# Two pairs of heads scored inside the value unit of the third attention, and its first two probabilities turned together

## Chip, cores and metric

The kernel runs on one core of a Trainium2 chip. The metric is the device time of one launch in microseconds; lower is better. Engines: PE (TensorE, matrix products), DVE (VectorE), ACT (ScalarE), POOL (GpSimd), and SP, whose queue issues the loads of the weights.

## What is computed

A network of two blocks over 256 latent rows and 256 context rows of width 1024, in float32. The first block has two layers; each layer projects the normalised rows, runs three attentions next to each other and merges them. The third one is what the change touches: 16 query heads of width 64 over 4 key heads, with a window of 128 positions and a learned "sink" term in the softmax. Cut to its core:

```python
sq_l, sk_l, sv_l = swa_heads(sq_l, sk_l, sv_l, rope_hd)      # rotated queries and keys, 16 / 4 heads
sq_c, sk_c, sv_c = swa_heads(sq_c, sk_c, sv_c, None)         # the same of the context, not rotated
# latent queries: all context keys, and latent keys within the window
s_loc = jnp.where(mask, jnp.einsum('bqhgd,bkhd->bhgqk', qg, kb), NEG_INF)
s_ctx = jnp.einsum('bqhgd,bkhd->bhgqk', qg, k_ctx)
p_ctx, p_loc = sink_softmax(sink, (s_ctx, s_loc))
o = einsum('bhgqk,bkhd->bqhgd', p_ctx, v_ctx) + einsum('bhgqk,bkhd->bqhgd', p_loc, vb)
# context queries (layer 0 only): context keys alone
(p,) = sink_softmax(sink, (einsum(qg, k_ctx),));  o = einsum(p, v_ctx)
```

The second block (four mixers with large matrix products) is not touched.

## The kernel before

**Order of the work.** `plan()` (lines 163 to 379) writes one list of steps. Each engine's program walks this list and does its own part of each step, in order; semaphores tie the engines together. Nothing is scheduled at run time: an engine that waits holds up all that stands behind it on its queue. The step `gemm` is a unit of matrix product: weights of 256 rows and up to 512 columns at a time (a chunk) are loaded by SP, split into a high part by ACT (line 1749) and a low part by DVE (line 2380), and used by PE in three products (high by high, low by high, high by low; lines 1211 to 1213, 1248 to 1250).

**Banks.** The product memory has eight banks of 128 x 512 float32. PE takes one with `take(pool, key)` (line 1056), which goes round the pool's banks in turn and waits until the bank's last content has been read. The pools overlap:

```python
POOL = {"wide": (0, 1, 2, 3), "turn": (4, 5), "out": (6, 7), "turn4": (4, 5, 6, 7), "out_turned": (6,), "back": (7,)}
```

**In front of the third attention** (lines 285 to 292): the keys `sk`, the queries `sq` in two units of four blocks (two heads each), and the value unit `sv`. The units of kind "rope" leave their result with heads across the partitions. The second, `sq` with j = 1, holds all four banks of "turn4". Their blocks are then rotated one after the other (step `rotate`): ACT writes the swapped halves into a slot of `stage` (line 1815), DVE makes the cosine product (line 2467) and with it gives the bank back, POOL multiplies by the sines and adds (lines 849, 852), ACT makes the high part (line 1823), POOL the low part (line 858). PE meanwhile works on `sv`: four chunks for four row tiles, in the four banks of "wide", and ACT copies these to `v` at the end (line 1897).

**The third attention** (`attend` with r = 2). An item is one query tile and one head; layer 0 has 4 x 16 (the tiles of the context see 256 keys, those of the latent rows 512), layer 1 has 2 x 16 with 512 keys. Per item: scores on PE, two heads at a time in two halves of the array and in two banks (lines 1476, 1479, 1482); the negated row maximum with mask and sink on DVE, in one instruction (line 2925); the exponential with row sum on ACT (line 2171), which gives the bank back; the turning (transposes) of the probabilities on PE (line 1318) into a bank of "turn"; its copy to `probs_turned` on DVE for even items (line 2942) and on ACT for odd ones (line 2192); and the product with V on PE (line 1529) for two heads together. Turnings run LAG = 3 items behind the scores, products with V PV_LAG = 5 behind.

**The start.** The first `FIRST` = 2 items are ahead of the others. PE issues their scores inside `sv`, before its third chunk (line 1174), into "turn4" banks. DVE and ACT have the step `attend_first` for them, which stands ahead of the step of `sv` on their queues. All later items are in the step `attend` behind `sv`, with scores in "wide" banks. So the order on PE, with S01 for the scores of items 0 and 1 and T0 for the turning of item 0, is: two chunks of `sv`, S01, two chunks of `sv`, S23, T0, S45, T1, T2, S67, the first product with V, T3, and so on.

Of the kernel before, what the change touches and what calls it, by code (L numbers as in the profile page):

```python
# [56 lines left out]
LAG = 3  # L57
PV_LAG = LAG + 2
PT_SLOTS = {0: 3, 1: 3, 2: 4}
NM_RING = 32  # L60
FIRST = 2
B_LAG = 3
EARLY_BY = (16, 17)

# [98 lines left out]
def plan():  # L163

    steps, chunks, to_split = [], [], []
# [37 lines left out]
    for l in (0, 1):  # L203
        qt = ALL_TILES if l == 0 else LAT_TILES
# [70 lines left out]
            gemm("value", ("dv", l, j), ALL_TILES, ("h", l), w_in, D, OFF_DV + 512 * j, 512, j=j,  # L275
                 head=(l, 1, qt) if j else None, pool="wide" if j else "turn4")
        scored = len(qt) * HEADS[1]
        steps.append(("attend", l, 1, qt, FIRST, scored))
        steps.append(("head_squares", l, qt[:-1]))
        steps.append(("attend", l, 1, qt, scored))  # L280
        steps.append(("head_squares", l, qt[-1:]))
# [125 lines left out]
def program(nc, dram, out, known):  # L407
    ctx = ExitStack()
    with ctx:
        S = Signals(nc, ctx, known)  # L410
        steps, chunks, to_split = plan()
# [139 lines left out]
        def probs_at(r, i):  # L551

            return stage(i) if r == 1 else STG[:, 512 * ((i + 4) % 6):512 * ((i + 4) % 6) + 512]
# [176 lines left out]
        def squares(t):  # L730

            return QT[:, :, P * t:P * t + P]

        def items(l, r, qt):
            return [(t, h) for t in qt for h in range(HEADS[r])]

# [311 lines left out]
        def _(pe):  # L1048
# [7 lines left out]
            def take(pool, key):  # L1056

                b = POOL[pool][turns[pool] % len(POOL[pool])]
                turns[pool] += 1
                if uses[b]:  # L1060
                    pe.wait_ge(*S.nth(f"bank{b}_emptied", uses[b]))
                uses[b] += 1
                S.use_bank(key, b, uses[b])
                return b
# [78 lines left out]
            def gemm(u, turned):  # L1143
# [27 lines left out]
                for n, (src, k0, kt, col, width) in enumerate(u.chunks):  # L1171
                    while late and late[0][0] <= n:
                        turn(*late.pop(0)[1])
                    if u.more.get("head") and n == (2 if u.key[0] == "sv" else 1):
                        l, r, qt = u.more["head"]
                        attend(l, r, qt, 0, FIRST)
                    if turned and turns_inside(u) and n == len(u.chunks) - 1:
                        turn_qk(turned)
                    if u.more.get("tail") and n in (1, 2):
                        l, r, qt = u.more["tail"]  # L1180
                        done = len(items(l, r, qt))
                        if n == 1:
                            attend(l, r, qt, done, done + LAG)
                        else:
                            attend(l, r, qt, done + LAG, done + PV_LAG)
                    if u.more.get("tail") and n == 3 and u.more["r"] == 2:
                        turn_inverses(u.more["l"])
                    c = u.at[n]
                    pe.wait_ge(*S.at("w_low", c))
                    slot = part_of[c] % PART_SLOTS  # L1190
                    for t in u.tiles:
                        if n == 0:
                            open_banks[t] = take(u.more.get("pool", "wide"), (u.key, t))
                        b = open_banks[t]
                        for kk in range(kt):
                            k = k0 + kk
                            once(left_ready(u.left, k, t))
                            high, low = left_high_low(u.left, k, t)
                            o = banks[b][:, 0:width]
                            if u.more.get("across"):  # L1200
                                a = u.more.get("first", 0)
                                high, low = (part[:, a:512] for part in left_all(u.left, k))
                                block = slice(P * t, P * t + P)
                                o = banks[b][:, a:512]
                                wh, wl = WH[:, slot, kk, block], WL[:, slot, kk, block]
                                pe.matmul(o, wh, high, start=(k == 0), stop=False)  # L1206
                                pe.matmul(o, wh, low, start=False, stop=False)  # L1207
                                mm = pe.matmul(o, wl, high, start=False, stop=(k == u.kt - 1))  # L1208
                                continue
                            wh, wl = WH[:, slot, kk, 0:width], WL[:, slot, kk, 0:width]  # L1210
                            pe.matmul(o, high, wh, start=(k == 0), stop=False)  # L1211
                            pe.matmul(o, high, wl, start=False, stop=False)  # L1212
                            mm = pe.matmul(o, low, wh, start=False, stop=(k == u.kt - 1))  # L1213
                        if n == len(u.chunks) - 1:
                            mm.then_inc(*fills(b))
                            if t == u.tiles[-1]:
                                S.same("w_used", c, f"bank{b}_filled")
                        elif t == u.tiles[-1]:
                            mm.then_inc(*S.up("w_used", c))
# [222 lines left out]
            def attend_first(l, r, qt):  # L1442
                pass

            def attend(l, r, qt, start=FIRST, stop=None):
                todo = items(l, r, qt)
                width = VALUE[r]
                for i in range(start, stop or len(todo)):
                    if r == 0 and i % 2 == 0 and i < len(todo):
                        for n in (i, i + 1):  # L1450
                            t, h = todo[n]
                            nk = P * len(key_tiles(t))
                            qk_ready(l, r, t, h)
                            b = take("turn4" if i < FIRST else "wide", ("s", l, r, t, h, 0))
                            high, low = (part[:, n % 2, :] for part in q_pair(n))
                            k_high, kl = KH[0:MQ, h, 0:nk], mla_k_low(l, h, slice(0, MQ), nk)
                            pe.matmul(banks[b][:, 0:nk], high, k_high, start=True, stop=False)
                            pe.matmul(banks[b][:, 0:nk], low, k_high, start=False, stop=False)
                            pe.matmul(banks[b][:, 0:nk], high, kl, start=False, stop=True).then_inc(*fills(b))
                    if r and i < len(todo):  # L1460
                        t, h = todo[i]
                        nk = P * len(key_tiles(t))
                        qk_ready(l, r, t, h)
                        if r == 1 or h % 2 == 0:
                            halves = [(h, 0), (h, 1)] if r == 1 else [(h, 0), (h + 1, 0)]
                            two = [take("turn4" if i < FIRST else "wide", ("s", l, r, t, hh, m)) for hh, m in halves]
                            hq, hk = (h, h) if r == 1 else (h // 2, h // 4)
                            q_high = QH[:, hq, P * t:P * t + P]
                            ql = q_low(l, r, hq, 1, t).rearrange("p a c -> p (a c)")
# [10 lines left out]
                            for m, b in enumerate(two):  # L1480
                                a = slice(64 * m, 64 * m + 64)
                                pe.matmul(banks[b][:, 0:nk], q_high[a], kl[m], start=False,  # L1482
                                          stop=True).then_inc(*fills(b))
                    if r == 2 and i % 2 == 0 and PV_LAG < i < len(todo):
                        pair_values(l, todo, i - PV_LAG - 1)
                    if LAG <= i < len(todo) + LAG:
                        t, h = todo[i - LAG]
                        pe.wait_ge(*S.at("probs", (l, r, t, h)))
                        pr = probs_at(r, i - LAG)
                        turn(("pt", l, r, t, h), [(pr[:, P * n:P * n + P], P * n) for n in range(len(key_tiles(t)))])  # L1490
                    if r == 2 and i % 2 == 0 and i >= len(todo):
                        pair_values(l, todo, i - PV_LAG - 1)
                    if r < 2 and i >= PV_LAG:
                        n_item = i - PV_LAG
# [227 lines left out]
        def _(act):  # L1722
# [416 lines left out]
            def attend_first(l, r, qt):  # L2139
                if r < 2:  # L2140
                    load_table(ACT.Exp)
                if r == 1:
                    act.wait_ge(*S.at("rope_parted", (("dk", l, 1), 3)))
                attend(l, r, qt, 0, FIRST)

            def attend(l, r, qt, start=FIRST, stop=None):
                todo = items(l, r, qt)
                ring = 4 if r == 1 else 6
                if r == 2 and start:
# [1 line left out]
                for i in range(start, stop or len(todo) + (LAG if r < 2 else PV_LAG + 1)):  # L2151
                    if i == (len(todo) // 2 if l and r < 2 else len(todo)):
                        prepare(by_key[("z", l, r, 0 if r else 1)].pfirst + PART_SLOTS)
                    if r == 2 and i % 8 == 4 and i > 8:
                        save_out(l, *todo[i - PV_LAG])
                    if r == 2 and LAG <= i < len(todo) + LAG and (i - LAG) % 2:
                        turned(l, r, todo, i - LAG)
                    if i < len(todo):
                        t, h = todo[i]
                        nk = P * len(key_tiles(t))  # L2160
# [196 lines left out]
        def _(dve):  # L2357
# [545 lines left out]
                                    SCALE[3] if which == 0 else 1.0, ALU.mult, ALU.mult).then_inc(*S.empties(key))  # L2903

            def attend_first(l, r, qt):
                attend(l, r, qt, 0, FIRST)

            def attend(l, r, qt, start=FIRST, stop=None):
                todo = items(l, r, qt)
                last_in_group = lambda n: todo[n][1] % GROUP[r] == GROUP[r] - 1  # L2910
                for i in range(start, stop or len(todo) + PV_LAG + (2 if r < 2 else 0)):
# [19 lines left out]
                            mx.then_inc(*S.up("neg_max", key))  # L2931
                    if r == 1 and 1 <= i < len(todo):
                        combine(l, i - 1, *todo[i - 1])
                    if r != 1 and LAG <= i < len(todo) + LAG and (i - LAG) % 2 == 0:
                        n = i - LAG
                        t, h = todo[n]
                        key = ("pt", l, r, t, h)
                        nk = P * len(key_tiles(t))
                        if n >= PT_SLOTS[r]:
                            dve.wait_ge(*S.at("pt_used", (l, r, n - PT_SLOTS[r])))  # L2940
                        dve.wait_ge(*S.filled(key))
                        v.tensor_copy(turned_at(r, n)[:, 0:nk], ps(key)[:, 0:nk]).then_inc(*S.empties(key))
# [323 lines left out]
```

## Time and profile before

| | us |
|---|---|
| median of 3 runs (2323.86 to 2324.48) | 2324.48 |
| the profiled execution | 2324.32 |
| its span, first to last instruction | 2322.5 |
| PE busy | 2303.3 |
| DVE busy | 1435.2 |
| ACT busy | 1256.7 |
| POOL busy | 321.0 |

The span is shorter than the execution's time by what lies before the first and behind the last instruction. Busy times overlap, since the engines work side by side. Matmuls are pipelined: one starts before the end of the one before it, so the distance between starts is what one costs, not its duration.

### The profile page before, as it was taken

The page shows a single profiled execution, that of the slowest core. Times are in us where ns is not written, and L with a number is a line of the kernel's source. Part 1 is how long each engine was busy: PE and PEld are TensorE (multiplying, and loading weights), DVE is VectorE, ACT ScalarE, POOL GpSimd, SP SyncE. Part 2 cuts the span into 40 slices and gives each one's busy share as a digit, 9 for nine tenths or more (in the row PEclk, how much of TensorE's full clock was granted, in tenths as well). Part 3 has the DMA queues.
Part 4 walks back from the last instruction along what each step waited for, and adds up shares of the span by engine and source line. Part 5 has one row for each costly group of instructions (what it writes and reads, how often), then busy time and mean ns, then how long its engine had stood idle before and what let it go on. Part 6 is the DMA issues. An engine that isn't in the chain of part 4 may idle for free.

```text
span 2322.5 us, 33979 instructions
## 1 busy us (share of the span) xinstructions
PE 2303.3 (99%) x12887; PEld 1929.6 (83%) x12887; DVE 1435.2 (62%) x2329; ACT 1256.7 (54%) x2371; POOL 321.0 (14%) x432
## 2 busy tenths in 40 slices
PE   8999999999999999999999999999999999999999
PEld 7998888788887888988878888888888888888887
DVE  4665654776647445765447566766589745465665
ACT  5553245753257333755756576565466565555653
POOL 2020033520130000020632221000010400000000
PEclk9999999999999999999999999999999999999999
DMA  8503553134540532426423616655555663655554
GB/s 265 136 25 107 160 160 109 38 122 133 154 109 2 137 127 73 128 80 195 118 73 109 173 55 182 217 190 180 183 167 180 191 188 99 197 176 178 190 177 132
DMA packets 175026, 326.05 MB, mean 140 GB/s; under 512 B 15718, under 2 KB 30176, under 8 KB 174224
## 3 DMA queue, kind: packets, MB, share of 16 engines
q1 hardware_dynamic: 167792, 301.58, 42.3%
q0 software_dynamic: 6496, 20.19, 3.4%
q8 instruction: 104, 1.70, 0.3%
q10 hardware_dynamic: 576, 2.10, 0.3%
q14 instruction: 58, 0.48, 0.1%
HBM read 316.68 MB, written 3.21 MB: 138 GB/s over the span
## 4 chain that ended last, share of the span: by engine, by line
PE 93%; DVE 3%; ACT 2%; issue 1%; DMA 1%; POOL 0%; SPq 0%; DVEq 0%; ACTq 0%; POOLq 0%
PE bank L1211 16%; PE bank L1213 16%; PE bank L1212 16%; PE bank L1318 6%; PE bank L1206 5%; PE bank L1208 5%; PE bank L1207 5%; PE bank L1250 3%; PE bank L1248 3%; PE bank L1249 3%; PE bank L1506 3%; PE bank L1529 2%; PE bank L1476 1%; PE bank L1482 1%; PE bank L1479 1%
## 5 line engine op out<-in xcount | busy, mean ns | idle before, releaser
L2380 DVE TENSOR_TENSOR w_low_part<-w_raw,w_high_part 128x1024 fp32r<-128x1024 f32 (+3 forms) x544 | 645.2, 1200 | 514.0 <-ACT w_high_part L1749 509.7
L1749 ACT ACTIVATE w_high_part<-w_raw 128x1024 fp32r<-128x1024 f32 (+3 forms) x544 | 552.1, 1029 | 601.7 <-PE bank L1213 360.5
L1211 PE MATMUL bank<-w_high_part,h_high 128*128 128x512 f32 (+3 forms) x1376 | 529.3, 385 | 1.0 <-DVE w_low_part L2380 0.6
L1213 PE MATMUL bank<-w_high_part,h_low 128*128 128x512 f32 (+3 forms) x1376 | 523.6, 381 | 0.0
L1212 PE MATMUL bank<-w_low_part,h_high 128*128 128x512 f32 (+3 forms) x1376 | 523.1, 380 | 0.0
L1211 PEld LDWEIGHTS bank<-w_high_part,h_high 128*128 128x128 f32 x1376 | 258.7, 188 | 51.7 <-DVE w_low_part L2380 2.8
L1213 PEld LDWEIGHTS bank<-w_high_part,h_low 128*128 128x128 f32 x1376 | 258.5, 188 | 48.6
L1212 PEld LDWEIGHTS bank<-w_low_part,h_high 128*128 128x128 f32 x1376 | 258.8, 188 | 46.3
L2171 ACT ACTIVATE stage<-bank,neg_max 128x512 f32<-128x512 f32 (+1 forms) x240 | 146.9, 617 | 61.0 <-DVE neg_max L2930 55.2
L1248 PE MATMUL bank<-h_high,w_high_part 128*128 128x512 f32 (+1 forms) x416 | 148.6, 357 | 0.0
L1250 PE MATMUL bank<-h_high,w_low_part 128*128 128x512 f32 (+1 forms) x416 | 148.3, 357 | 0.0
L1249 PE MATMUL bank<-h_low,w_high_part 128*128 128x512 f32 (+1 forms) x416 | 148.3, 356 | 0.0
L1318 PE MATMUL bank<-ident,stage 128*128 128x128 f32 (+1 forms) x824 | 124.8, 279 | 1.1 <-ACT stage L2171 0.4
L1206 PE MATMUL bank<-h_high,w_high_part 128*128 128x512 f32 (+1 forms) x320 | 118.9, 372 | 0.0
L1208 PE MATMUL bank<-h_high,w_low_part 128*128 128x512 f32 (+1 forms) x320 | 117.8, 368 | 0.0
L1207 PE MATMUL bank<-h_low,w_high_part 128*128 128x512 f32 (+1 forms) x320 | 117.7, 368 | 0.0
L1318 PEld LDWEIGHTS bank<-ident,stage 128*128 128x128 f32 (+1 forms) x824 | 92.2, 140 | 28.8 <-issue 17.0
L2930 DVE TENSOR_REDUCE neg_max<-bank 128x1 f32<-128x512 f32 (+1 forms) x144 | 81.0, 597 | 42.1 <-PE bank L1482 29.9
L1211 PE MATMUL bank<-w_high_part,wide_high 128*128 128x512 f32 x224 | 88.2, 394 | 0.0
L1249 PEld LDWEIGHTS bank<-h_low,w_high_part 128*128 128x128 f32 x416 | 78.6, 189 | 11.3
L1250 PEld LDWEIGHTS bank<-h_high,w_low_part 128*128 128x128 f32 x416 | 78.6, 189 | 11.2
L1248 PEld LDWEIGHTS bank<-h_high,w_high_part 128*128 128x128 f32 x416 | 78.6, 189 | 11.1
(439 smaller groups left out, 4013.5 us busy)
## 6 DMA issues: line engine op xcount, KB each, us to landing
w_raw<-in_w_in_dram SPq DMA_DIRECT2D x160, 512.0 KB, 3.7
w_raw<-in_a_w_in_dram SPq DMA_DIRECT2D x96, 512.0 KB, 4.3
w_raw<-in_b_w_in_dram SPq DMA_DIRECT2D x80, 512.0 KB, 4.3
w_raw<-in_w_branch_dram SPq DMA_DIRECT2D x48, 512.0 KB, 3.9
w_raw<-in_w_mod_dram SPq DMA_DIRECT2D x37, 512.0 KB, 3.9
w_raw<-in_a_w_out_dram SPq DMA_DIRECT2D x32, 512.0 KB, 4.5
w_raw<-in_c_w_in_dram SPq DMA_DIRECT2D x32, 512.0 KB, 4.2
w_raw<-in_w_out_dram SPq DMA_DIRECT2D x16, 512.0 KB, 3.8
```

The source lines that it names most:

```text
L1206: pe.matmul(o, wh, high, start=(k == 0), stop=False)
L1207: pe.matmul(o, wh, low, start=False, stop=False)
L1208: mm = pe.matmul(o, wl, high, start=False, stop=(k == u.kt - 1))
L1211: pe.matmul(o, high, wh, start=(k == 0), stop=False)
L1212: pe.matmul(o, high, wl, start=False, stop=False)
L1213: mm = pe.matmul(o, low, wh, start=False, stop=(k == u.kt - 1))
L1248: pe.matmul(o, wh, high, start=(k == 0), stop=False)
L1249: pe.matmul(o, wh, low, start=False, stop=False)
L1250: mm = pe.matmul(o, wl, high, start=False, stop=(k == u.kt - 1))
L1318: mm = pe.transpose(order(banks[b][0:m, col:col + p]), src, IDENT[0:p, 0:p])
L1749: nc.scalar.activation(WH[:, n % PART_SLOTS, 0:kt, 0:width], raw[:, 0:kt, 0:width], ACT.Copy).then_inc(*S.up("w_high", c))
L2380: v.tensor_tensor(WL[:, s, 0:kt, 0:width], raw[:, 0:kt, 0:width], WH[:, s, 0:kt, 0:width].bitcast(F32), ALU.subtract).then_inc(*S.up("w_lo ...
```

## The change

A second constant holds how many items each attention scores ahead. It is 2 for the first two attentions, as before, and 4 for the third. Three things follow for the third attention. The scores of items 2 and 3 are issued with those of 0 and 1 inside `sv`, into "turn4" banks; DVE's and ACT's parts of them move with them, ahead of `sv`'s own steps. `turned_in` gives the items that are turned at a step of the loop: as before at all steps but the first of `attend`, where items 0 and 1 are turned together. And the order on PE becomes: two chunks of `sv`, S01, S23, two chunks of `sv`, S45, T0, T1, T2, S67, and as before from there.

```diff
+FIRST_OF = {0: 2, 1: 2, 2: 4}
@@ steps
-        steps.append(("attend", l, 1, qt, FIRST, scored))
+        steps.append(("attend", l, 1, qt, FIRST_OF[1], scored))
@@ program
+        def turned_in(r, i, count):
+
+            if i == FIRST_OF[r] > LAG:
+                return range(0, i - LAG + 1)
+            return range(i - LAG, i - LAG + 1) if max(LAG, FIRST_OF[r]) <= i < count + LAG else ()
@@ PE, gemm
-                        attend(l, r, qt, 0, FIRST)
+                        attend(l, r, qt, 0, FIRST_OF[r])
@@ PE, attend
-            def attend(l, r, qt, start=FIRST, stop=None):
+            def attend(l, r, qt, start=None, stop=None):
+                start = FIRST_OF[r] if start is None else start
-                            two = [take("turn4" if i < FIRST else "wide", ("s", l, r, t, hh, m)) for hh, m in halves]
+                            two = [take("turn4" if i < FIRST_OF[r] else "wide", ("s", l, r, t, hh, m)) for hh, m in halves]
-                    if LAG <= i < len(todo) + LAG:
-                        t, h = todo[i - LAG]
+                    for n_item in turned_in(r, i, len(todo)):
+                        t, h = todo[n_item]
                         pe.wait_ge(*S.at("probs", (l, r, t, h)))
-                        pr = probs_at(r, i - LAG)
+                        pr = probs_at(r, n_item)
@@ ACT, attend
-                attend(l, r, qt, 0, FIRST)
+                attend(l, r, qt, 0, FIRST_OF[r])
-                    if r == 2 and LAG <= i < len(todo) + LAG and (i - LAG) % 2:
-                        turned(l, r, todo, i - LAG)
+                    for n in turned_in(r, i, len(todo)) if r == 2 else ():
+                        if n % 2:
+                            turned(l, r, todo, n)
@@ DVE, attend
-                attend(l, r, qt, 0, FIRST)
+                attend(l, r, qt, 0, FIRST_OF[r])
-                    if r != 1 and LAG <= i < len(todo) + LAG and (i - LAG) % 2 == 0:
-                        n = i - LAG
+                    for n in turned_in(r, i, len(todo)) if r != 1 else ():
+                        if n % 2:
+                            continue
                         t, h = todo[n]
```

## Rows read from the trace of the kernel before

**Rows 1.** The page, part 1: busy us, share of the span, instructions.

```profile
PE 2303.3 (99%) x12887; PEld 1929.6 (83%) x12887; DVE 1435.2 (62%) x2329; ACT 1256.7 (54%) x2371; POOL 321.0 (14%) x432
```

**Rows 2.** Waits of PE, whole span: us in total, times, longest.

```profile
PE bank L1476 <- ACT stage L2171: 2.7, 6, 0.9
...
PE bank L1476 <- ACT v L1897: 0.9, 2, 0.6
```

**Rows 3.** Groups by line and form: busy, mean ns, idle before and releaser.

```profile
L2942 DVE COPY probs_turned<-bank 128x512 f32<-128x512 f32 x48 | 33.1, 690 | 33.4 <-PE bank L1318 33.4
```

**Rows 4.** Timeline of PE, layer 0, head in sv: start, duration, what.

```profile
679.62 0.39 PE L1476 MATMUL bank<-k_high,q_high 64*128 64x256 f32 x2
...
680.18 0.39 PE L1211 MATMUL bank<-w_high_part,h_high 128*128 128x256 f32 x1
```

**Rows 5.** Timelines of DVE, then ACT, layer 0, the rotation's last blocks.

```profile
679.85 0.41 DVE L2467 SCALAR_TENSOR_TENSOR stage<-bank,rope_hd 128x256 f32<-128x256 f32 x1
...
682.24 0.42 DVE L2467 SCALAR_TENSOR_TENSOR stage<-bank,rope_hd 128x256 f32<-128x256 f32 x1
...
684.55 0.48 DVE L2925 CUSTOM_DVE_ANT_0 bank<-bank,v,neg_sink 128x256 f32<-128x256 f32 x1
...
680.33 1.54 ACT L1815 ACTIVATE stage<-bank 32x256 f32<-32x256 f32 x4
```

**Rows 6.** Timeline of PE, layer 0, end of sv and start.

```profile
685.91 0.28 PE L1213 MATMUL bank<-w_high_part,h_low 128*128 128x256 f32 x1
686.82 0.39 PE L1476 MATMUL bank<-k_high,q_high 64*128 64x256 f32 x2 [0.64 <-ACT v L1897]
...
688.30 0.94 PE L1318 MATMUL bank<-ident,stage 128*128 128x128 f32 x4
689.26 0.39 PE L1476 MATMUL bank<-k_high,q_high 64*128 64x256 f32 x2
...
690.40 0.66 PE L1318 MATMUL bank<-ident,stage 128*128 128x128 f32 x4
690.98 0.39 PE L1476 MATMUL bank<-k_high,q_high 64*128 64x256 f32 x2
```

**Rows 7.** Timelines of ACT, then DVE, layer 0, the same stretch.

```profile
686.04 1.19 ACT L1897 COPY v<-bank 128x256 f32<-128x256 f32 x4
...
687.45 0.49 DVE L2925 CUSTOM_DVE_ANT_0 bank<-bank,v,neg_sink 128x256 f32<-128x256 f32 x1 [1.95 <-PE bank L1482]
...
688.26 0.42 DVE L2942 COPY probs_turned<-bank 128x256 f32<-128x256 f32 x1
```

**Rows 8.** Timeline of PE, layer 1, head and start.

```profile
1347.23 0.50 PE L1476 MATMUL bank<-k_high,q_high 64*128 64x512 f32 x2
...
1348.12 0.39 PE L1211 MATMUL bank<-w_high_part,h_high 128*128 128x256 f32 x1
...
1354.07 0.50 PE L1476 MATMUL bank<-k_high,q_high 64*128 64x512 f32 x2
...
1357.25 0.63 PE L1318 MATMUL bank<-ident,stage 128*128 128x128 f32 x4 [0.15 <-DVE probs_turned L2942]
1357.81 0.50 PE L1476 MATMUL bank<-k_high,q_high 64*128 64x512 f32 x2
```

**Rows 9.** Timelines of DVE, then ACT, layer 1, rotation and start.

```profile
1348.04 0.42 DVE L2467 SCALAR_TENSOR_TENSOR stage<-bank,rope_hd 128x256 f32<-128x256 f32 x1 [1.56 <-ACT stage L1815]
...
1355.07 0.76 DVE L2925 CUSTOM_DVE_ANT_0 bank<-bank,v,neg_sink 128x512 f32<-128x512 f32 x1 [2.68 <-PE bank L1482]
...
1356.42 0.69 DVE L2942 COPY probs_turned<-bank 128x512 f32<-128x512 f32 x1
...
1353.10 0.91 ACT L1897 COPY v<-bank 128x256 f32<-128x256 f32 x3
```

**Rows 10.** Windows: busy us per engine, granted clock, DMA share, GB/s.

```profile
core 0: us, PE busy (x) PEld busy (x) DVE busy (x) ACT busy (x) POOL busy (x), PEclk, DMA share, GB/s
22.10:25.50 3.40, 2.33 (x28) 1.29 (x32) 0.98 (x4) 1.80 (x4) 0.00 (x0) 1.00 1.05 388
25.60:29.00 3.40, 3.40 (x24) 1.54 (x16) 2.54 (x5) 1.29 (x4) 0.00 (x0) 0.50 1.05 387
```

More of the change, by code:

```diff
@@ L1453, in attend @@
                             qk_ready(l, r, t, h)
-                            b = take("turn4" if i < FIRST else "wide", ("s", l, r, t, h, 0))
+                            b = take("turn4" if i < FIRST_OF[r] else "wide", ("s", l, r, t, h, 0))
                             high, low = (part[:, n % 2, :] for part in q_pair(n))
@@ L2143, in attend_first, with attend @@
                     act.wait_ge(*S.at("rope_parted", (("dk", l, 1), 3)))
-                attend(l, r, qt, 0, FIRST)
-            def attend(l, r, qt, start=FIRST, stop=None):
+                attend(l, r, qt, 0, FIRST_OF[r])
+            def attend(l, r, qt, start=None, stop=None):
+                start = FIRST_OF[r] if start is None else start
                 todo = items(l, r, qt)
@@ L2905, in attend_first, with attend @@
             def attend_first(l, r, qt):
-                attend(l, r, qt, 0, FIRST)
-            def attend(l, r, qt, start=FIRST, stop=None):
+                attend(l, r, qt, 0, FIRST_OF[r])
+            def attend(l, r, qt, start=None, stop=None):
+                start = FIRST_OF[r] if start is None else start
                 todo = items(l, r, qt)
```

## The prediction

> **What bounds the kernel now.** I read the page first: the PE row shows it busy for 2303.3 of 2322.5 us [rows 1], so only some 19 us are not PE's own work, and any change to the order of work can win only from those. Then the waits of PE over the whole span: at the score matmuls (line 1476) they amount to 2.7 us behind exponentials and 0.9 us behind the copy of V [rows 2]; the third attention's share of that is small and sits at its two starts. Last the timelines of both starts, layer 0 (all four query tiles, 256 keys in the first ones) and layer 1 (two tiles, 512 keys). Once the attention runs, VectorE waits for PE before its copies of turned probabilities (33.4 us over 48 of the wide ones, all behind line 1318, [rows 3]) and not the other way round. So PE sets the beat, and two items of lead for ACT and VectorE are worth nothing there; what can change is the start.
>
> Names: S01, S23, S45, S67 are the scores of the four first pairs of heads, T0, T1, T2 the turnings of the first probabilities.
>
> **The change part by part.** No instruction is added or removed. On PE, S23 (six matmuls) moves from behind the value unit `sv` into it, right behind S01; T0 moves behind S45 and next to T1. The minima (VectorE) and exponentials (ACT) of items 2 and 3 move ahead of ACT's copies of V. No DMA moves: SP's queue and its waits are the same, POOL's only dependent is the sink sum, which waits for item 7. Each edit is weighed at its layer, by end points: when S67 starts before and after. From S67 on both orders are the same.
>
> *Which banks S23 now takes.* The four scores now all come from the pool "turn4", banks 4 to 7. The unit in front, `sq` with j = 1, takes its four blocks from the same pool, one bank each. S01 takes the banks of blocks 0 and 1, which is what it does today. S23 takes those of blocks 2 and 3, and they are given back only when VectorE has done the rotation's cosine product (line 2467) of that block. Both banks are taken before the first of the six matmuls, and PE works its queue in order: behind the waiting S23 stand the rest of `sv` (two of four chunks) and everything after, and nothing else on PE can go ahead. Before, S23 took "wide" banks, those of V.
>
> *Layer 0, the head.* S01 starts at 679.62 and `sv` goes on at 680.18, so a pair of scores costs 0.56 us and S23 would start at 680.18 [rows 4]. Block 2 was given back at 679.85 + 0.41 = 680.26. ACT makes the swapped halves of block 3 from 680.33 for 1.54 us, and VectorE's product of it runs from 682.24 for 0.42 us [rows 5]: the bank is free at 682.66. A handover from another engine to PE costs 0.14 us more: the second V copy ends about 0.27 + 0.37 us after 686.04, at 686.68, and PE starts at 686.82 [rows 6, 7]. So S23 starts at 682.80: a new wait of 2.62 us in which PE has nothing. This chain (ACT, VectorE) doesn't depend on anything PE does after 680, so it comes no sooner. `sv` goes on at 682.80 + 0.56 = 683.36 instead of 680.18, 3.18 us later.
>
> *Layer 0, the start.* `sv`'s last matmul starts at 685.91 [rows 6], now at 689.09, and S45 0.21 us behind it (the step from such a matmul to scores), at 689.30. The V copies are no bar any more: VectorE takes the minima from 684.55 on [rows 5] at 0.41 us each, so that the exponentials of four items are through by about 687.2, two us before `sv` ends. T0 comes at 689.86. T2 would be due 0.58 us later (four transposes take 690.40 to 690.98, [rows 6]), at 690.44; but it takes T0's bank, and VectorE's copy of T0 stands behind the minimum of item 4. That starts 0.63 us after its scores (687.45 behind 686.82), at 689.93, the copy 0.41 later, and takes 0.42 [rows 6, 7]: done 690.76, T2 at 690.90, a wait of 0.46 us. S67 follows 0.30 later at 691.20. Today it starts at 689.26: **+1.9 us**. In pieces: added 2.62 + 0.46; gone the wait of S23 for V (686.82 against 686.12, 0.70), T2's wait for the exponential of item 2 (0.38: T1 and T2 take 688.30 to 689.26, where 0.58 would do) and one change between scores and turnings (0.08).
>
> *Layer 1.* The pair of 512 keys costs 1348.12 - 1347.23 = 0.89 us [rows 8]. Here no modulation sums delay the rotation: VectorE's last product starts at 1348.04 and ends at 1348.46 [rows 9], so S23 starts at 1348.60 in place of 1348.12, a wait of 0.48. What stands at 1354.07 today (S23) becomes S45 at 1354.07 + 0.89 + 0.48 = 1355.44. ACT's V copies start at 1353.10 today and two more exponentials of 0.68 stand before them now, so the second copy ends at about 1355.1 [rows 9] and, with the handover, at 1355.24: covered, with 0.2 us to spare, and every 0.1 us beyond that would cost 0.1. VectorE's minimum of item 4 starts 1.00 behind its scores (1355.07 behind 1354.07), 1356.44; the copy 0.67 later, 1357.11, for 0.69: T2 at 1357.94, and S67 0.56 behind at 1358.50. Today 1357.81 [rows 8, 9]: **+0.7 us**.
>
> *Bank rotation between the two starts.* Two more takes from "turn4" shift its turn by two banks from here to layer 1's start, where two more bring it back. Layer 1's first two attentions and units then meet other neighbours in banks 4 to 7. No row of before shows that; the nearest are the two waits for a bank or a score at this start, 0.7 and 0.4 us. I bound it by -0.4 and +0.7 and take 0, as every taker of these banks waits for data made well after the earlier user left.
>
> Sum: 1.9 + 0.7 = 2.6 us. The profiled execution took 2324.32 us, 1.8 of it outside the span of 2322.5, and is 0.16 below the median of the three runs, 2324.48. Everything behind each start is PE's beat, so I carry the sum to the end undiminished: 2326.9 by its own time, 2327.1 by the median. Forecast **2327.1 us**, its own range 2326.0 to 2328.3.
>
> **The rivals.** *The wait in the head is not there.* If blocks 2 and 3 were free, only the other terms stand: layer 0 -1.16 + 0.46 = -0.7, layer 1 +0.7 - 0.5 = +0.2, together -0.5: 2324.0. For it: it is what the edit needs in order to bring anything. Against it: the bank order and the 682.66.
>
> *PE's clock falls.* The slower side. The new idle spell of 2.6 us is the longest after the start of the kernel; the longest that rows 2 show is 0.9. In the window 22.1 to 25.5 PE had light work and was busy for 2.33 of 3.40 us, and the next 3.4 us went at a granted clock of 0.50, 1.2 GHz, before it was back at 2.4 GHz [rows 10]. A fall behind the head of layer 0 would make 3.4 us of PE-bound work at half speed: 1.7 us lost per such stretch, 2328.8. Against it: before and behind the spell stand dense matmuls, unlike there. It decides against "no change" from a second stretch on (2.6 + 3.4 = 6.0, 2330.5), since 0.2% is 4.65 us.
> The Trainium skill (TensorE: Matmul & The Clock Gate, Part 1, on the HAM clock gate) has the rule that idle spells between bursts of matmuls send the clock back to 1.2 GHz; by that rule this change could cost the stretch above besides the wait, and the trace shows such a fall only at the light start, not at the short waits of the attentions.
>
> *The shift of banks bites in layer 1.* +0.7 as bounded: 2327.8.
>
> **How the numbers follow.** Forecast 0.70; no wait in the head 0.10; clock falls for one stretch 0.10, for two 0.03; bank shift 0.07. Faster or slower by over 0.2% (4.65 us) is what a measurement of this kernel can tell from no change. The faster case stays 4 us short of it: 0.02 for what I don't see. Slower needs the second stretch, or one and 0.4 us more: 0.05. Within 0.2%: 0.93. The range takes in the faster case's edge, the bank bounds and one stretch of slow clock: 2324.3 to 2329.2.
>
> **What would show it.** Right: a PE idle spell of about 2.6 us before the second L1476 group of layer 0's head and 0.5 in layer 1, released by VectorE's line 2467; no idle before S45 for V (line 1897); T2 released by VectorE's line 2942 in both layers; S67 1.9 and a further 0.7 later relative to S01; granted clock 1.00 there. Wrong: S23 straight behind S01 in layer 0; a stretch at 0.50; a difference that first appears at another stage.

## The result, and the profile after

The changed kernel takes 2328.49 us (median of 20 runs, 2326.58 to 2330.04), the kernel before 2324.12 beside it (20 runs; all but one, at 2329.52, between 2323.86 and 2324.55): +4.37 us, a ratio of 1.0019, 95% interval 1.0013 to 1.0025. The forecast of 2327.1 is 1.4 us short of it; the range holds it. As a change it foretold 2.6 us and is 1.8 short, since the three runs it started from had a median of 2324.48, 0.36 above that of the 20. The median hides more than it tells, since the times of the changed kernel stand in three groups:

```
2326.58 2326.89 2326.91 2327.02          4 runs
2328.16 to 2328.56                       7 runs
2329.41 to 2330.04                       9 runs
```

The profiled execution, 2328.16 us (span 2326.4), is one of the middle group. First its waits of PE (line waited at, releaser: us in total, times, longest). Lines 1476, 1318, 2467, 2942 and 1897 of the kernel before are now 1484, 1325, 2477, 2954 and 1905.

```profile
PE bank L1484 <- DVE stage L2477: 3.0, 2, 2.6
PE bank L1325 <- DVE probs_turned L2954: 0.9, 2, 0.5
PE bank L1484 <- ACT v L1905: 0.2, 1, 0.2
```

The wait for the rotation's banks is new: 3.0 us over two times, one a layer. The wait of scores for V has shrunk from 0.9 [rows 2] to 0.2: the 0.64 in front of S23 is gone. The wait of a turning for VectorE's copy stands in both layers. Next PE's timeline in layer 0, from S01 to S67:

```profile
679.18 0.39 PE L1484 MATMUL bank<-k_high,q_high 64*128 64x256 f32 x2
...
682.37 0.39 PE L1484 MATMUL bank<-k_high,q_high 64*128 64x256 f32 x2 [2.57 <-DVE stage L2477]
...
683.80 0.41 PE L1218 MATMUL bank<-w_high_part,h_high 128*128 128x256 f32 x1
684.01 0.41 PE L1219 MATMUL bank<-w_low_part,h_high 128*128 128x256 f32 x1
684.23 0.41 PE L1220 MATMUL bank<-w_high_part,h_low 128*128 128x256 f32 x1
...
685.72 0.41 PE L1218 MATMUL bank<-w_high_part,h_high 128*128 128x256 f32 x1
...
686.54 0.28 PE L1220 MATMUL bank<-w_high_part,h_low 128*128 128x256 f32 x1
686.65 0.29 PE L1218 MATMUL bank<-w_high_part,h_high 128*128 128x256 f32 x1
686.78 0.28 PE L1219 MATMUL bank<-w_low_part,h_high 128*128 128x256 f32 x1
...
690.34 0.39 PE L1484 MATMUL bank<-k_high,q_high 64*128 64x256 f32 x2
...
691.97 0.41 PE L1325 MATMUL bank<-ident,stage 128*128 128x128 f32 x2 [0.42 <-DVE probs_turned L2954]
692.31 0.39 PE L1484 MATMUL bank<-k_high,q_high 64*128 64x256 f32 x2
```

S01, then 2.57 us of nothing, then S23, as foretold. But look at the distance between the starts of the value unit's matmuls: 0.21 or 0.22 us from 683.80 on, 0.12 from 686.5 on. The same instruction at two speeds is PE at 1.2 and at 2.4 GHz. The windows of the changed kernel say so (columns as in [rows 10]):

```profile
679.20:682.40 3.20, 0.63 (x9) 0.46 (x8) 1.39 (x4) 3.11 (x8) 2.82 (x5) 1.00 0.58 166
682.40:685.80 3.40, 3.40 (x19) 3.19 (x20) 2.94 (x9) 1.96 (x7) 3.06 (x3) 0.56 0.18 23
685.80:689.20 3.40, 3.40 (x29) 3.40 (x29) 0.06 (x1) 1.38 (x6) 0.00 (x0) 0.94 0.38 136
```

PE is busy for 0.63 us of the first 3.20, and of the next 3.40 most go at a granted clock of 0.5 (the window's mean is 0.56, since the slow stretch begins at about 683.0 and ends at about 686.2). Layer 1, S01 to S67, has the waits and no slow clock:

```profile
1351.73 0.50 PE L1484 MATMUL bank<-k_high,q_high 64*128 64x512 f32 x2 [0.46 <-DVE stage L2477]
...
1361.08 0.63 PE L1325 MATMUL bank<-ident,stage 128*128 128x128 f32 x4 [0.52 <-DVE probs_turned L2954]
1361.64 0.51 PE L1484 MATMUL bank<-k_high,q_high 64*128 64x512 f32 x2
```

Where the time went, by the end points that the prediction used: S01 to S67 takes 13.13 us in layer 0, 9.64 before [rows 4, 6]: +3.49. In layer 1, from S01 at 1350.31, 11.33 against 10.58 [rows 8]: +0.75. Between the two, S67 of layer 0 to S01 of layer 1, 658.00 against 657.97: nothing. S01 of layer 0 came 0.44 earlier. That is no effect of the change: S01 lies between 679.2 and 679.8 in all profiled executions but that of experiment 11, which moves it. Nor does it follow the half-clock stretches at the kernel's start, of which [rows 10] show one and this execution has none: it is 679.65 in experiment 4, without any, and 679.42 in experiment 2, with two. 3.49 + 0.75 + 0.03 - 0.44 = 3.8 of the spans' 3.9 us.

### The profile page after: what moved, and what is told of

Same layout as the page of the kernel before. It is cut to its first block, busy times and chain, and to the rows that moved or that the text cites. A ratio compares the mean times of both kernels' runs of the same rounds, so it can differ in the third digit from the quotient of the medians.

```text
span 2326.4 us, 33979 instructions
## 1 busy us (share of the span) xinstructions
PE 2301.9 (99%) x12887; PEld 1929.1 (83%) x12887; DVE 1435.7 (62%) x2329; ACT 1260.0 (54%) x2371; POOL 321.0 (14%) x432
## 4 chain that ended last, share of the span: by engine, by line
PE 92%; DVE 3%; ACT 3%; issue 1%; DMA 1%; POOL 1%; SPq 0%; DVEq 0%; ACTq 0%; POOLq 0%
PE bank L1218 16%; PE bank L1220 16%; PE bank L1219 16%; PE bank L1325 6%; PE bank L1213 5%; PE bank L1215 5%; PE bank L1214 5%; PE bank L1255 3%; PE bank L1256 3%; PE bank L1257 3%; PE bank L1514 3%; PE bank L1537 2%; PE bank L1484 1%; PE bank L1490 1%; PE bank L1487 1%
```

## The experiments

All were timed in five rounds, with 5 to 11 runs each; "before" is 2324.29 (33 runs) beside the first four, 2324.38 (33) beside the next four, 2324.10 (14) beside the next three and 2324.27 (15) beside the last. The theory: two new waits a layer as foretold, and PE's clock falls behind the long one, for no, one or two stretches, which makes the three groups.

**1. The changed kernel once more.**

> The changed kernel once more. Theory (two waits of 2.6 and 0.5 us in the heads, and a fall of PE's clock behind the first of them in most runs): the times stand on levels, 2326.8 with no fall, 2328.3 with one, and the highest 2329.7; a run on the highest level shows two stretches at a granted clock of 0.50. Rival (the upper levels come from the start of the kernel, where loads land sooner or later): the upper levels appear with the clock at 1.00 in layer 0's head, and PE's first long waits differ instead.

Measured: 2328.31 us, ratio 1.0016 (1.0008 to 1.0025): 4 runs at 2326.6 to 2327.0, 5 at 2327.9 to 2328.6, 2 at 2329.5 and 2329.7. The profile is of 2329.65. Its windows:

```profile
679.20:682.40 3.20, 0.89 (x9) 0.55 (x8) 1.41 (x4) 3.08 (x9) 2.75 (x4) 0.99 0.55 166
682.60:686.00 3.40, 3.35 (x17) 3.16 (x18) 2.87 (x8) 1.95 (x7) 3.10 (x3) 0.50 0.17 25
686.00:689.40 3.40, 3.40 (x19) 3.40 (x19) 0.14 (x2) 0.89 (x4) 0.00 (x0) 0.54 0.38 134
```

Twice 3.4 us at 1.2 GHz, behind the same wait: this run of the highest group has two stretches there. S01 to S67 of layer 0 takes 14.45 us (679.47 to 693.92), 1.32 more than with one stretch. This execution has two more such stretches at the kernel's start, but so has that of experiment 2, which stands in the lowest group; those cost nothing that the times show. The other runs have no trace, only a mean granted clock on record, from which one stretch anywhere takes 0.0007. Of the 31 runs of this kernel, the 20 of the result and these 11, all eight of the lowest group have 1.000, the twelve of the middle 0.998 or 0.999, and the eleven of the highest 0.997 or 0.998. So the lowest runs had no stretch at all, at the start neither, and the groups follow the clock. Whether a fall at the start and one in the head come together for a reason stays open.

**2. The idle time filled.** 20 matmuls of 256 columns that nobody reads, written into the first of S23's two banks before the second is taken (3 in layer 1):

```diff
+ if r == 2 and i == 2 and hh == 2:
+     for _ in range(3 if l else 20):
+         pe.matmul(banks[two[0]][:, 0:256], HH[:, 0, 0:P], HH[:, 0, 0:256], start=True, stop=True)
```

> The changed kernel, but PE doesn't sit idle in the heads: before it takes the bank of block 3 it issues matmuls of 256 columns (0.12 us each) into the bank of block 2 that nothing reads, 20 in layer 0 (2.4 us) and 3 in layer 1 (0.36 us). Theory (idle time makes the clock fall): every run on the lowest level, 2326.8 within 0.3, clock 1.00 in the heads, S23 at the same moment as in the changed kernel. Rival (the clock falls for another reason, or the upper levels have nothing to do with it): 2328.3 and 2329.7 appear as often as before, 16 of 20.

Measured: 2327.06 us (2326.82 to 2327.38), ratio 1.0012 (1.0003 to 1.0021). All 11 runs stand in the lowest group. Timeline of PE, and the window that was slow in the changed kernel:

```profile
680.22 2.63 PE L1479 MATMUL bank<-h_high 128*128 128x256 f32 x20 [0.17 <-DVE stage L2482]
682.78 0.39 PE L1489 MATMUL bank<-k_high,q_high 64*128 64x256 f32 x2
```

```profile
682.40:685.80 3.40, 3.40 (x30) 3.13 (x30) 2.76 (x9) 1.95 (x6) 3.21 (x4) 1.00 0.12 14
```

S23 starts no sooner than before (682.78, the fillers even end a little late), yet the window goes at clock 1.00 with 30 matmuls where 19 fitted. So the slow clock comes of PE's idleness and not of the order of the work. This is the experiment that settles the 1.4 us between the medians of the two kernels. The start of the profiled execution had two slow stretches, between 23.8 and 34.0 us, and its time of 2327.07 is in the lowest group all the same. One window of them:

```profile
27.20:30.60 3.40, 3.40 (x28) 1.13 (x21) 1.69 (x3) 2.20 (x5) 0.00 (x0) 0.50 1.06 384
```

**3 and 4. One layer alone.** Four items ahead only in layer 0, then only in layer 1, the other as before.

```diff
- FIRST_OF = {0: 2, 1: 2, 2: 4}
+ FIRST_OF = {0: 2, 1: 2, (2, 0): 4, (2, 1): 2}   # and the other way round
```

> Only layer 0 scores four items ahead; layer 1 is as in the kernel before. Theory: +1.9 for the waits, and the clock falls in most runs as in the whole change: levels 2326.1, 2327.6, 2329.0. Rival (the highest level needs both layers): the highest level is missing.

> Only layer 1 scores four items ahead; layer 0 is as in the kernel before. Theory: +0.7, 2324.9, and no fall of the clock, as the head's wait is 0.5 us only. Rival (layer 1 makes a stretch of slow clock too): some runs at 2326.3.

Measured: layer 0 alone 2327.86 us, ratio 1.0015 (1.0006 to 1.0024), in three groups again (2326.26; nine at 2327.71 to 2328.27; 2329.11). Layer 1 alone 2324.90 (2324.63 to 2325.18), ratio 1.0003 (0.9994 to 1.0012), one group. +0.6 for layer 1, against +0.75 in the timeline; 2326.26, a single run, is +2.0 for layer 0 without a stretch. The sum of the waits is as worked out, and each layer does its part alone.

**5. The second pair before the fourth chunk of `sv`.** By then the banks are free:

```diff
- attend(l, r, qt, 0, FIRST_OF[r])
+ attend(l, r, qt, 0, 2)
+ if u.key[0] == "sv" and n == 3:
+     attend(*u.more["head"], 2, FIRST_OF[2])
```

> S01 stays before the third chunk of the value unit, S23 goes before the fourth, 2.9 us later, when block 3's bank is free in both layers. Theory: no wait in the heads, no fall of the clock. But ACT now makes four exponentials before its V copies, and in layer 0 they end at 687.0, so S45 waits about 1.1 us for the second copy; T2 still waits 0.5 behind the minimum of item 4. Worked out: layer 0 +0.4, layer 1 +0.5, 2325.0, every run on one level. Rival (the value unit itself is slowed by the scores inside it, and not by the bank): 2326.8 or more, with levels.

Measured: 2325.34 us (2324.98 to 2325.56), ratio 1.0004 (0.9995 to 1.0013), one group: no head wait, no slow clock. It is still 1.0 above the kernel before. Timeline of PE, layer 0:

```profile
683.32 0.39 PE L1486 MATMUL bank<-k_high,q_high 64*128 64x256 f32 x2
...
687.81 0.39 PE L1486 MATMUL bank<-k_high,q_high 64*128 64x256 f32 x2 [0.82 <-ACT v L1907]
...
689.41 0.41 PE L1327 MATMUL bank<-ident,stage 128*128 128x128 f32 x2 [0.39 <-DVE probs_turned L2956]
```

The wait for V, which the changed kernel hid only because its head was 2.6 us late, is back at S45 with 0.82, and T2's wait stands.

**6. T0 in front of S45,** the rest as in the changed kernel, so that VectorE's copy of T0 comes before item 4's minimum. The core of it:

```diff
- if i == FIRST_OF[r] > LAG:
-     return range(0, i - LAG + 1)
- return range(i - LAG, i - LAG + 1) if max(LAG, FIRST_OF[r]) <= i < count + LAG else ()
+ return range(i - LAG, i - LAG + 1) if LAG <= i < count + LAG else ()
```

> The changed kernel with T0 in front of S45 on PE and its copy in front of the minimum of item 4 on VectorE, as in the kernel before. Theory: T2's waits of 0.4 and 0.5 us go, the head's waits and the falls of the clock stay: levels 0.9 below those of the changed kernel, 2325.9, 2327.4, 2328.8. Rival (T2 waits for something else, an exponential or ACT's copy of T1): the levels stay.

Measured: 2327.46 us, ratio 1.0014 (1.0005 to 1.0023), one run at 2325.41, six at 2327.15 to 2327.50, two at 2328.3 and 2328.5, two at 2329.4 and 2329.5. The last two are above every level that was worked out. The two lower groups lie 1.4 and 1.0 us below those of the changed kernel. The 0.9 us of waits of a turning for VectorE's copy are gone from the list, and S01 to S67 takes 12.52 us in layer 0 (679.61 to 692.13, again with one slow stretch) and 10.61 in layer 1 (1350.30 to 1360.91), 0.61 and 0.72 less than in the changed kernel. So this half of the title, the first two turnings together, cost 1.3 us: the 0.9 of waits and 0.2 a layer in the steps between scores and turnings, where the prediction had counted 0.08 as gained.

**7 and 8. What makes V late: the split of z's first weights?** ScalarE (1.05 us) and VectorE (1.23 us) split it into high and low parts inside the head. First the kernel before with that split behind the first items' exponentials; then this with the edits of 5 and 6.

```diff
- if b % 2:
+ if b % 2 and not (u.key[0] == "sq" and u.key[2] == 1 and b == 3):
      prepare(u.plast + PART_SLOTS + 1 + b // 2)
...
  attend(l, r, qt, 0, FIRST_OF[r])
+ if r == 2:
+     prepare(by_key["sv", l].plast + 2)
```

> The kernel before, with one step moved on ACT and VectorE: the split of the first weights behind the value unit stands behind the first items' minima and exponentials and no longer ahead of them. Theory (in layer 0 the V copies come late because VectorE splits weights from 683.3 to 684.6 before it takes the first minimum): S23's wait of 0.7 for V goes and T2's shrinks to 0.1, 2323.1. Rival (V copies are late for another reason): 2324.1.

> Four items ahead with all three repairs: S23 before the fourth chunk of the value unit, the weights' split behind the first items, T0 in front of S45. Theory: none of the waits of the start is left in either layer, -1.2 in layer 0 and -0.3 to -0.4 in layer 1, 2322.6, no fall of the clock. Rival (the lead of two more items is worth nothing in itself): not below the kernel before with the split moved alone, 2323.1.

Measured: 2324.02 us (2323.75 to 2324.41) and 2324.15 us (2323.84 to 2324.31), both with a ratio of 0.9999 (0.9990 to 1.0008). The theories missed by 0.9 and 1.5 us; the first run's time is that of its rival, though the split is the cause after all, as experiments 9 and 10 show. ScalarE's timeline of the second shows why:

```profile
685.35 0.48 ACT L2183 ACTIVATE stage<-bank,neg_max 128x256 f32<-128x256 f32 x1
...
685.80 1.07 ACT L1757 ACTIVATE w_high_part<-w_raw 128x1024 fp32r<-128x1024 f32 x1
686.75 1.20 ACT L1905 COPY v<-bank 128x256 f32<-128x256 f32 x4
```

The split only changed its place in the queue: it still stands ahead of the V copies, on which S45 waits (0.43 us at 687.54; in experiment 7 it is S23 that still waits, 0.48 us).

**9 and 10. The split out of the head** (its old place taken away as in 7), in front of the tenth item of the rotation; first in the kernel before, then with the edits of 5 and 6.

```diff
+ if r == 2 and i == 9:                       # ScalarE's and VectorE's loop
+     prepare(by_key["sv", l].plast + 2)
```

> The kernel before, with the split of z's first weights (about 1.05 us on ScalarE, 1.23 us on VectorE) taken out of the head altogether and put in front of the tenth item of the third attention, in both layers. Theory (in the head the split stands in ScalarE's queue between the first exponentials and the copies of V, so that the scores of the second pair and turning T2 come late): the head's waits of 0.70 and 0.38 us in layer 0 and 0.48 and 0.1 us in layer 1 shrink by about 1.5 us together, and what the rotation loses to the moved split decides: with TensorE 100% busy and ScalarE some 75 to 80% busy there, between 0 and 1.1 us a layer is given back. Time between 2322.7 and 2324.9, 2323.6 taken. Rival (V's copies are late for POOL or for their banks, not for the split): waits in the head stay as in the kernel before, time 2324.1 to 2326.3.

> The changed kernel with the scores of the second pair before the fourth chunk of sv, T0 in front of the third pair, and the split of z's first weights in front of the tenth item instead of behind the first four. Theory: with the split gone the copies of V start about 1 us earlier, the third pair's wait for V (0.43 us in layer 0, 0.46 us in layer 1 with the split behind the first items) and T1's delay behind VectorE's split (about 0.5 us) go, TensorE's clock does not fall: layer 0's S01 to S67 about 8.6 us against 9.64 of before, layer 1's about 10.2 against 10.58, minus 1.4 us in all, less what the rotation gives back (the same as in the run beside it, 0 to 1.1 us a layer): 2322.7 to 2324.9, 2323.2 taken, single level. Rival (it was never the split): 2324.1 as with the split behind the first items.

Measured: 2330.43 us (2329.61 to 2331.36), ratio 1.0028 (1.0017 to 1.0039), and 2330.29 (2329.52 to 2331.04), ratio 1.0027 (1.0016 to 1.0038). 6 us slower, outside what either theory gave. In the second the heads did what the theory said: S01 to S67 takes 8.59 us in layer 0 (679.77 to 688.36) and 10.27 in layer 1. In the first they gave less than half of the 1.5 us of its theory: 8.96 against 9.64 in layer 0 (679.38 to 688.34), and 10.58 as before in layer 1. No wait of these scores for V is left in either, so it was the split that held V up. The rest is in the rotation. VectorE, then PE, of the second:

```profile
693.58 1.23 DVE L2392 TENSOR_TENSOR w_low_part<-w_raw,w_high_part 128x1024 fp32r<-128x1024 f32 x1 [2.28 <-ACT w_high_part L1757]
694.72 0.49 DVE L2940 CUSTOM_DVE_ANT_0 bank<-bank,v,neg_sink 128x256 f32<-128x256 f32 x1
```

```profile
695.69 0.41 PE L1325 MATMUL bank<-ident,stage 128*128 128x128 f32 x2 [2.29 <-DVE probs_turned L2958]
```

VectorE's part needs ScalarE's, and ScalarE's stood a whole exchange behind: VectorE idled 2.28 us for it, with minima and copies queued behind the split; ScalarE then idled for those minima, and PE waited 2.29 and 2.04 us. And the clock fell behind these waits too, in the profile of the second:

```profile
696.50:699.90 3.40, 3.40 (x26) 2.39 (x24) 2.10 (x9) 2.60 (x11) 0.00 (x0) 0.55 0.37 138
1373.00:1376.40 3.40, 3.40 (x26) 2.86 (x24) 1.60 (x6) 1.66 (x5) 0.00 (x0) 0.55 0.00 1
```

In that of the first it fell only in layer 1; in layer 0, behind the same wait of 2.29 us, it stayed at 1.00:

```profile
696.80:700.20 3.40, 3.40 (x38) 2.45 (x36) 2.92 (x13) 2.93 (x12) 0.20 (x1) 1.00 0.31 116
```

**11. A longer wait:** the changed kernel with the four scores in front of the second chunk.

```diff
- if u.more.get("head") and n == (2 if u.key[0] == "sv" else 1):
+ if u.more.get("head") and n == 1:
```

> The changed kernel with the four items' scores one chunk of sv earlier (in front of the second chunk in place of the third), so that the wait of the second pair for the banks of sq's last blocks is longer: about 5.4 us in layer 0 and 3.3 us in layer 1 against 2.57 and 0.46. Theory (the wait comes in full, and TensorE idling between S01 and S23 is what brings the lower clock behind it): S01 to S67 grow by 2.8 us in each layer over the changed kernel's, 2326.9 + 5.7 = 2332.6 us without a stretch at half clock, and most runs carry one to four stretches of about 1.45 us each, now behind layer 1's head too: 2334 to 2338. Rival (the clock falls from something else at that place, which the four scores only uncover): layer 1 shows no stretch at 0.5, and the levels are 2332.6, 2334.1 and 2335.5.

Measured: 2336.46 us (2335.39 to 2337.76, 5 runs), ratio 1.0054 (1.0042 to 1.0067). PE, layer 0 and layer 1, then the window that ends with the first wait and the one behind the second:

```profile
682.53 0.58 PE L1484 MATMUL bank<-k_high,q_high 64*128 64x256 f32 x2 [5.43 <-DVE stage L2477]
...
1354.66 0.68 PE L1484 MATMUL bank<-k_high,q_high 64*128 64x512 f32 x2 [3.30 <-DVE stage L2477]
```

```profile
679.10:682.50 3.40, 0.00 (x0) 0.00 (x0) 1.51 (x4) 3.28 (x9) 2.85 (x4) 0.50 0.52 157
1354.90:1358.30 3.40, 3.40 (x16) 2.71 (x15) 2.82 (x6) 1.52 (x3) 3.27 (x4) 0.51 0.15 21
```

Both waits came out as worked out from the rotation's end, and layer 1, whose clock never fell behind 0.46 us, falls behind 3.30. That excludes the rival, that something else at layer 0's place does it. In layer 0 the clock fell inside the wait, so that one of its two stretches passed while PE had nothing to do.

**12. The split in the wide half of the rotation, VectorE's part behind ScalarE's.** Edits of 5 and 6, the split's old place taken away as in 7, and:

```diff
+ if r == 2 and i == len(todo) // 2 + 5:      # ScalarE; VectorE: + 8
+     prepare(by_key["sv", l].plast + 2)
```

> The split of the third pair's head as in the run before it with the tenth item (second pair before sv's fourth chunk, T0 in front of the third pair, z's first weights split in the rotation), but the split stands in the wide half of the rotation, and VectorE's part (low = raw - high, which waits for ScalarE's) three items behind ScalarE's part, so that neither engine waits for the other. Theory: the head's gain is kept (S01 to S67 8.6 us in layer 0 against 9.64 of before, 10.27 in layer 1 against 10.58, together -1.36 us); in the rotation the 2.3 and 2.0 us waits behind the split were mostly VectorE's wait for ScalarE and go, and of the 1.05 and 1.23 us that are left at most 0.5 us a layer comes through, the engines being 65 to 80% busy there; TensorE then has no wait of over 1 us there and its clock does not fall: 2322.8 to 2323.8, 2323.1 taken, one level. Rival (whatever is put into the rotation comes out of it at full length, since ScalarE and VectorE have no room there): +1.1 to 1.2 us a layer, 2324.9 to 2325.2 and the head's gain is lost.

Measured: 2322.78 us (2322.37 to 2323.06, 11 runs), against 2324.05 to 2324.44 of before. The ratio is 0.9994 and its interval, 0.9985 to 1.0003, reaches 1; but none of the 11 runs comes within 0.9 us of the fastest of the 15. Timeline of PE in layer 0, then ScalarE's and VectorE's split:

```profile
679.54 0.39 PE L1484 MATMUL bank<-k_high,q_high 64*128 64x256 f32 x2
...
688.12 0.39 PE L1484 MATMUL bank<-k_high,q_high 64*128 64x256 f32 x2
```

```profile
718.29 1.06 ACT L1757 ACTIVATE w_high_part<-w_raw 128x1024 fp32r<-128x1024 f32 x1
```

```profile
721.14 1.22 DVE L2392 TENSOR_TENSOR w_low_part<-w_raw,w_high_part 128x1024 fp32r<-128x1024 f32 x1
```

VectorE's row has no idle time in front of it now. S01 to S67: 8.58 us in layer 0, 10.27 in layer 1, 1.06 + 0.31 = 1.37 less than before, of which the medians show 1.49. PE's scores in the rotation go on at steps of 2.94 us past both splits. It is the one version that comes out below the kernel before, and it takes from the change only the early scores, not their place nor the double turning. Not all of the 1.37 us is theirs: the kernel before with the split out of its head (experiment 9) has 8.96 and 10.58, so moving the split alone brought 0.68 and the early scores 0.38 + 0.31 = 0.69. No run has the split moved this way without the early scores, so how the whole time divides wasn't measured.

## Why the prediction was right, and where not

**How much of it was luck.** The two waits that were to make the change are there in the sizes worked out, but the range held the median by chance in part. It was to take in one stretch of slow clock, and 9 of the 20 runs, those with two, lie above its edge of 2329.2; had two more runs of the middle group been among them, the median would have been outside.

**What bounds the kernel, and which banks S23 takes.** Right. The wait is there, released by the line named, and moves with the place of the scores (0.46 to 3.30 us and 2.57 to 5.43 us in experiment 11, none in experiment 5).

**The terms.** Layer 0's head 2.57 for 2.62 us, T2's wait 0.42 for 0.46, S45's wait for V gone. Layer 1: 0.46 for 0.48, T2's 0.52, the sum +0.75 for +0.7. Bank shift: 0.03 for 0. The sum of 2.6 holds wherever the clock does not fall: the four fastest runs, 2326.6 to 2327.0, are 2.5 to 2.9 above the 2324.12 of before, and the filled kernel 2.8 above its own. That their times are also the forecast of 2327.1 within 0.5 owes something to the 0.36 us by which it started too high.

**The step that failed** is the weight given to the rival "PE's clock falls". It had its place, its mechanism and its prices (2328.8 with one stretch, 2330.5 with two), and 0.13. It came in 16 of 20 runs, 9 of them with two stretches (by the groups; the profiles show one run each of the middle and the highest, the mean clocks of the others agree). "Against it: before and behind the spell stand dense matmuls, unlike there" was no reason: 2.6 us of idleness amid dense matmuls was enough in most executions. The rows that I compared it with, light work at the kernel's start [rows 10], show PE busy for 2.33 of 3.40 us ahead of a fall; here it was busy for 0.63 of 3.20 and I should have read that as more, not less, of a case. By the groups of runs, a forecast with one stretch, 2328.8, would have been the better one. The sign of being wrong that the prediction named, "a stretch at 0.50", did show.

**Its price** was mis-sized as well: 1.7 us a stretch came from half speed throughout. The medians of the groups, 2326.90, 2328.35 and 2329.73, lie 1.45 and 1.38 us apart. The timeline has the reason: the matmuls of 256 columns start 0.213 us apart when slow (683.80 to 685.72 is nine steps) and 0.120 when fast (686.54 to 686.78 is two), not half of 0.213; 3.4 us x (1 - 0.120 / 0.213) = 1.5.
The Trainium skill (TensorE: Matmul & The Clock Gate, Part 1, under the heading on 56 and 53.3 ns) has a small fixed cost in each matmul that shows only at the faster clock; the trace agrees in kind and not in size, with 0.120 against 0.213 / 2 = 0.107: 13 ns over half, where the page has about 2.5 ns.

**Why it wasn't 0 or faster.** The edit was to hide the start's waits for V and for exponentials, 1.1 us in layer 0. It hid them, but behind a 2.6 us hole in front of `sv`'s second half, and the double turning put VectorE's copy behind a minimum, which with the changed steps around it cost 1.3 us over both layers. Experiments 5, 6 and 12 take these apart. Not settled is why a given execution gets no, one or two stretches: the same code does all three.

## What to carry to other kernels

When work is moved ahead into another unit, ask first who still holds the buffers that it takes, and until when: the place of the scores relative to the rotation's end was worth 2.6 us, the overlap itself 0.7 over both layers (experiment 12 against experiment 9). On a kernel that is bound by TensorE, price every new idle spell of a few us twice, once for itself and once for a stretch at 1.2 GHz behind it (at 0.5 to 0.8 us none was seen, at 2.0 to 2.6 us in most cases), and look at all timings, not at their median: groups that lie a fixed step apart are that stretch coming and going. A producer and consumer pair on two engines (high part, low part) that is put into a rotation of both has to be staggered: put at the same item it cost waits of 2.3 and 2.0 us and the slow clock behind them, three items apart and among wider items nothing that the rows show (which of the two did it wasn't taken apart).

## What the runs showed of the hardware

- Granted clock: 2.57 us of idle PE between dense matmuls brought one or two stretches of 3.4 us at 1.2 GHz in 16 of 20 runs (by the groups and mean clocks; two profiles show the stretches themselves); 2.0 to 2.3 us, inside the rotation, did so in three of the four waits that the profiles of experiments 9 and 10 hold. 0.46 and 0.82 us never did: the 22 runs with only such waits (experiments 4 and 5) stand in one group each. In the wait of 5.43 us the clock fell before the wait was over.
- 20 unread matmuls in the wait, which took 2.63 us, kept the clock at 1.00 behind it in the profiled run and all 11 runs in the lowest group, and cost 0.2 us.
- One stretch costs 1.3 to 1.5 us where PE sets the pace with matmuls of 256 columns (1.45 and 1.38 between the groups, 1.32 between two profiles), not half of its 3.4. Two at the kernel's start, in the profiled run of experiment 2, cost nothing that the times show.
